# Stick-breaking attention by sigmoids and a scan of products, with the weights' products shared between GpSimd and VectorE

## The reference

```python
for i in range(seq // Q_BLOCK):                       # Q_BLOCK = 128, seq = 512
    z = jnp.einsum('bqhd,bkhd->bhqk', q[:, q0:kv_len], k[:, :kv_len]).astype(jnp.float32) * scale
    causal = k_pos < q_pos
    log_beta = jax.nn.log_sigmoid(z)
    log_1m = jnp.where(causal, log_beta - z, 0.0)
    later = lax.cumsum(log_1m, axis=3, reverse=True) - log_1m
    w = jnp.where(causal, jnp.exp(log_beta + later), 0.0)
    outs.append(jnp.einsum('bhqk,bkhd->bqhd', w.astype(v.dtype), v[:, :kv_len]))
```

## Time and profile before

| | |
|---|---|
| median of 3 runs (lowest, highest) | 1973.13 us (1972.97, 1973.66) |
| the profiled execution, its own time | 1974.07 us |
| its span, from first to last instruction | 1972.3 us |
| TensorE busy | 1940.5 us, 98% |
| VectorE busy | 1470.6 us, 75% |
| ScalarE busy | 953.6 us, 48% |
| GpSimd busy | 454.8 us, 23% |
| mean granted clock of TensorE | 0.997 |

### The profile page before, as it was taken

One profiled execution on the slowest core, in us unless ns is written; L12 is line 12 of the kernel. 1 busy time (PEld: TensorE's weight loads), 2 busy tenths in 40 slices (PEclk: granted clock), 3 DMA queues, 4 the chain that ended last, 5 costly groups with the idle time before them and its releaser, 6 DMA issues.

```text
span 1972.3 us, 27125 instructions
## 1 busy us (share of the span) xinstructions
PE 1940.5 (98%) x10176; PEld 1582.1 (80%) x10176; DVE 1470.6 (75%) x2123; ACT 953.6 (48%) x1541; POOL 454.8 (23%) x471
## 2 busy tenths in 40 slices
PE   9999999999999999999999999999999999999997
PEld 6777878898897776787889889788888888886666
DVE  8995477877785449757786778778778778437985
ACT  5574343333344348733333335565555555236774
POOL 4131100570171000010066036124333331000002
PEclk9999999999999999999999999999999999999998
DMA  8465322243233220022324224322222223322112
GB/s 291 112 140 161 106 77 97 64 145 92 75 108 117 87 95 11 1 88 86 99 75 145 86 70 115 91 71 59 86 85 77 81 65 107 98 79 72 36 38 75
DMA packets 84546, 180.57 MB, mean 92 GB/s; under 512 B 18240, under 2 KB 33984, under 8 KB 84416
## 3 DMA queue, kind: packets, MB, share of 16 engines
q1 hardware_dynamic: 80848, 172.08, 29.1%
q0 software_dynamic: 3424, 6.23, 1.2%
q10 hardware_dynamic: 144, 0.52, 0.1%
HBM read 171.53 MB, written 7.27 MB: 91 GB/s over the span
## 4 chain that ended last, share of the span: by engine, by line
PE 68%; DVE 18%; ACT 6%; issue 6%; DMA 1%; SPq 0%; DVEq 0%; ACTq 0%
PE psum L522 12%; PE psum L525 12%; PE psum L523 12%; DVE wl L418 3%; ACT wh L406 3%; PE psum L462 3%; PE psum L459 3%; PE psum L460 3%; PE psum L563 2%; PE psum L566 2%; PE psum L564 2%; PE psum L544 2%; PE psum L1090 1%; PE psum L1092 1%; PE psum L1091 1%
## 5 line engine op out<-in xcount | busy, mean ns | idle before, releaser
L418 DVE TENSOR_TENSOR wl<-raw,wh 128x1024 fp32r<-128x1024 f32 (+3 forms) x359 | 430.8, 1203 | 255.1 <-ACT wh L406 254.2
L522 PE MATMUL psum<-xh,wh 128*128 128x512 f32 x1376 | 543.2, 395 | 1.8 <-DVE xl L641 1.8
L525 PE MATMUL psum<-xh,wl 128*128 128x512 f32 x1376 | 537.0, 390 | 2.5 <-DVE wl L418 2.5
L523 PE MATMUL psum<-xl,wh 128*128 128x512 f32 x1376 | 535.7, 389 | 0.0
L406 ACT ACTIVATE wh<-raw 128x1024 fp32r<-128x1024 f32 (+3 forms) x359 | 345.0, 964 | 291.1 <-PE psum L525 98.9
L522 PEld LDWEIGHTS psum<-xh,wh 128*128 128x128 f32 x1376 | 258.4, 188 | 61.2 <-ACT wh L406 2.6
L525 PEld LDWEIGHTS psum<-xh,wl 128*128 128x128 f32 x1376 | 258.3, 188 | 60.2 <-DVE wl L418 6.3
L523 PEld LDWEIGHTS psum<-xl,wh 128*128 128x128 f32 x1376 | 258.4, 188 | 55.2 <-issue 2.4
L431 POOL TENSOR_TENSOR raw<-raw 128x256 f32<-128x256 f32 x78 | 74.0, 949 | 441.1 <-DMA raw<-d_w 441.1
L462 PE MATMUL psum<-fh,wl 128*128 128x256 f32 x546 | 154.9, 284 | 1.8 <-DVE wl L418 1.6
L459 PE MATMUL psum<-fh,wh 128*128 128x256 f32 x546 | 154.7, 283 | 1.2 <-DVE fl L965 1.0
(11 more groups left out here) (548 smaller groups left out, 3710.3 us busy)
## 6 DMA issues: line engine op xcount, KB each, us to landing
raw<-d_w SPq DMA_DIRECT2D x224, 512.0 KB, 3.6
raw<-d_w SPq DMA_DIRECT2D x126, 256.0 KB, 2.7
Mt<-d_kd SPq DMA_DIRECT2D x64, 64.0 KB, 2.5
raw<-d_w SPq DMA_DIRECT2D x8, 320.0 KB, 2.9
bc<-d_bc SPq DMA_DIRECT2D x8, 256.0 KB, 4.5
d_ud<-ust SPq DMA_DIRECT2D x8, 256.0 KB, 2.6
U<-d_ud POOLq DMA_DIRECT2D x64, 32.0 KB, 2.4
d_yd<-HY SPq DMA_DIRECT2D x64, 32.0 KB, 2.1
```

Source lines behind the costliest of these rows:

```text
L418: dve.e.tensor_tensor(K.wl[n % NH][:, 0:w], K.raw[n % RAW][:, o:o + w], K.wh[n % NH][:, 0:w].bitcast(F32), ALU.subtract).then_inc(K.S["lo" ...
L522: pe.e.matmul(b[:, :], WH[:, o:o + P], XH, start=(k == k0), stop=False)
L523: pe.e.matmul(b[:, :], WH[:, o:o + P], XL, start=False, stop=False)
L525: mm = pe.e.matmul(b[:, :], WL[:, o:o + P], XH, start=False, stop=(k == k1 - 1))
```

## The change

The attention now has 32 steps n = 4 p + i, one for a pair of heads p and a block of 128 queries i, with queries in the partitions and 128 (i + 1) keys along the row, for both heads. Per step:

- TensorE, `scores_pe(n)`: two products and two masks into banks 0, 1 or 2, 3 in turn, which it may take when the scans of step n - 2 are done ("rem").
- ScalarE, `sigmoid_act(n)`: beta = sigmoid(z) into one of three buffers (the third is `xs`), which it may write when the turn of step n - 3 is done ("trn"); then sigmoid(-z) in place in PSUM.
- VectorE, `remain_dve(n)`: a reversed scan of products over each head's row gives the share left (`left`, two buffers), first head 1, then head 0; then it multiplies beta of head 1 by the share left.
- GpSimd, `weigh_pool(n)`: multiplies beta of head 0 by the share left.
- TensorE, `turn1_pe(n)`: 2 (i + 1) transposes into banks 4 and 5, which it may take when the copy of step n - 1 is done ("wg"). ScalarE, `turned_act(n)`: copies them into `ww` (two buffers). After each fourth turn, `mix_pe(p)` as before.

Sums, splits, absolute values, Exp and Ln are gone. ScalarE loads the table of the sigmoid before step 0, and at t = 4 the table of Ln and Exp for `head_rsqrt_act(3)` and the sigmoid's again; the second FFN starts with the table of Ln and Exp, which before was still loaded from the attention. The queues run through t = 2 to 31 with scores t, turn t - 3 and, where t is divisible by 4, a mix. The last mix stands after five of eight steps of b_w_o.

```diff
-def sums_pe(K, pe, p, part):
...
-def softplus_act(K, act, i):
...
-def weigh_act(K, act, i):
...
-def softplus_abs_dve(K, dve, p):
...
-def softplus_dve(K, dve, i):
...
+TURN_BANK, SPREAD_BANK = 4, 6
+def score_bank(n):
+    return 2 - n % 2 * 2
+def keys(n):
+    return P * (n % 4 + 1)
+def scores(K, n):
+    b = score_bank(n)
+    return K.psum[:, b:b + 2, 0:keys(n)]
+def beta(K, n):
+    return K.beta[n % 3].rearrange("p (e c) -> p e c", e=2)[:, :, 0:keys(n)]
...
+def scores_pe(K, pe, n):
+    p, i = n // 4, n % 4
     pe.wait_ge("kq", 8 + p + 1)
+    pe.wait_ge("mk", 4)
     for e in range(2):
+        take(pe, score_bank(n) + e, ("rem", 2 * n + 1))
+    for e in range(2):
+        r = slice(64 * e, 64 * e + 64)
+        pe.e.matmul(scores(K, n)[:, e, :], K.qT[r, p, i * P:(i + 1) * P], K.kT[r, p, 0:keys(n)], start=True, stop=False,
+                    skip_group_check=True)
+    for e in range(2):
+        mm = pe.e.matmul(scores(K, n)[:, e, i * P:(i + 1) * P], K.mkb[:, :], K.idb[:, :], start=False, stop=True,
                          skip_group_check=True)
     mm.then_inc(K.S["sc"], 1)
+def sigmoid_act(K, act, n):
+    z = scores(K, n)
+    act.wait_ge("sc", n + 1)
+    act.wait_ge("trn", n - 2)
+    act.other("sigmoid")
+    act.e.activation(beta(K, n), z, ACT.Sigmoid).then_inc(K.S["act"], act.up())
+    act.e.activation(z, z, ACT.Sigmoid, scale=-1.0).then_inc(K.S["sgm"], 1)
+def remain_dve(K, dve, n):
+    z, out = scores(K, n), K.left[n % 2]
+    dve.wait_ge("sgm", n + 1)
+    dve.wait_ge("wgt", n - 1)
+    dve.wait_ge("mk", 4)
+    k = keys(n)
+    none = K.zero[:, 0:1].broadcast_to([P, k])
+    dve.e.tensor_tensor_scan(out[:, 1, 0:k][:, ::-1], z[:, 1, :][:, ::-1], none, 1.0, ALU.mult, ALU.add).then_inc(
+        K.S["dve"], dve.up())
+    scanned = dve.n
+    dve.e.tensor_tensor_scan(out[:, 0, 0:k][:, ::-1], z[:, 0, :][:, ::-1], none, 1.0, ALU.mult, ALU.add).then_inc(
+        K.S["rem"], 1)
+    dve.wait_ge("dve", scanned)
+    w = beta(K, n)[:, 1, 0:k - 1]
+    dve.e.tensor_tensor(w, w, out[:, 1, 1:k], ALU.mult).then_inc(K.S["rem"], 1)
+def weigh_pool(K, pool, n):
+    k = keys(n)
+    w = beta(K, n)[:, 0, 0:k - 1]
+    pool.wait_ge("rem", 2 * n + 1)
+    pool.e.tensor_tensor(w, w, K.left[n % 2][:, 0, 1:k], ALU.mult).then_inc(K.S["wgt"], 1)
+def turn1_pe(K, pe, n):
     for e in range(2):
+        take(pe, TURN_BANK + e, ("wg", n + 1))
+    pe.wait_ge("wgt", n + 1)
+    pe.wait_ge("rem", 2 * n + 2)
     for e in range(2):
+        for j in range(n % 4 + 1):
+            c = slice(j * P, (j + 1) * P)
+            mm = pe.e.transpose(K.bank[TURN_BANK + e][:, c], beta(K, n)[:, e, c], K.con("ident"))
+    mm.then_inc(K.S["trn"], 1)
+def turned_act(K, act, n):
+    p, i = n // 4, n % 4
+    act.wait_ge("trn", n + 1)
+    act.wait_ge("mix", p - 1)
+    act.wait_ge("hbc", 16)
+    act.e.activation(K.ww[:, p % 2, :, i:4 * i + 1:3, :],
+                     K.psum[:, TURN_BANK:TURN_BANK + 2, 0:keys(n)].rearrange("p e (j c) -> p e j c", c=P),
+                     ACT.Copy).then_inc(K.S["wg"], 1)
...
 def att1_pe(K, pe):
...
+    for t in range(2, 32):
+        scores_pe(K, pe, t)
+        if t == 2:
             head_sums_pe(K, pe, 3, 7)
+        if t in LATE_HEADS:
+            head_spread_pe(K, pe, 3, LATE_HEADS[t], SPREAD_BANK)
+        if t >= 3:
+            turn1_pe(K, pe, t - 3)
+        if t % 4 == 0 and t >= 8:
+            mix_pe(K, pe, t // 4 - 2)
+    turn1_pe(K, pe, 29)
     x = x_of(K, pe, 5)
     last = product_steps(K, pe, "b_w_o", (0, 1), (2, 3), x, (("h", 17), ("h", 18)))
+    next(last)
+    turn1_pe(K, pe, 30)
+    mix_pe(K, pe, 6)
+    next(last)
+    next(last)
+    turn1_pe(K, pe, 31)
+    next(last)
+    next(last)
     mix_pe(K, pe, 7)
...
 def att1_act(K, act):
...
+    for t in range(2, 35):
+        if t < 32:
+            sigmoid_act(K, act, t)
+        if t == 4:
             head_rsqrt_act(K, act, 3)
+        if t >= 3:
+            turned_act(K, act, t - 3)
+        if t % 4 == 1 and t >= 9:
+            mixed_act(K, act, t // 4 - 2)
     mixed_act(K, act, 7)
```

More of the change, by code:

```diff
@@ L345 @@
     + ["gcp", "conv", "fa", "gv", "fh", "fl"]
-    + ["hcp", "hsq", "hn", "hny", "hbc", "kq", "mk", "sc", "sp2", "spa", "spl", "sums", "wg", "mix", "vt"]
+    + ["hcp", "hsq", "hn", "hny", "hbc", "kq", "mk", "sc", "sgm", "rem", "wgt", "trn", "wg", "mix", "vt"]
     + ["mraw", "dtk", "mxs", "mset", "mseta", "msetp", "mci", "mcv", "mth", "mfin", "mz", "mzt", "mcbp", "mcb", "mtp", "mxt"]
@@ L1271, in sums_pe @@
     for e in range(2):
-        pe.e.matmul(z[:, e, :], own, A[0][:, e, :], start=False, stop=False, skip_group_check=True)
-    pe.wait_ge("spl", i + 3)
-    for e in range(2):
-        mm = pe.e.matmul(z[:, e, :], own, A[1][:, e, :], start=False, stop=True, skip_group_check=True)
-    mm.then_inc(K.S["sums"], 1)
+        for j in range(n % 4 + 1):
+            c = slice(j * P, (j + 1) * P)
+            mm = pe.e.transpose(K.bank[TURN_BANK + e][:, c], beta(K, n)[:, e, c], K.con("ident"))
+    mm.then_inc(K.S["trn"], 1)
@@ L1309, in weigh_act @@
-def weigh_act(K, act, i):
-    act.wait_ge("sums", i + 1)
-    act.wait_ge("mix", i // 3)
-    act.wait_ge("hbc", 16)
-    act.e.activation(part_of(K.ww, i), part_psum(K, i), ACT.Exp).then_inc(K.S["wg"], 1)
 def mixed_act(K, act, p):
@@ L1375, in att1_pe @@
         product(K, pe, "b_w_q", n - 8, 4 + n % 4, x, ("hcp", n + 1),
[L1376 removed]
+                between=(2, lambda K, pe: scores_pe(K, pe, 0)) if n == 14 else None)
         if n == 12:
@@ L1512, in att1_pool @@
 def att1_pool(K, pool):
+    for n in range(32):
+        weigh_pool(K, pool, n)
     add_squares(K, pool, 3)
@@ L3418, in att1_tensors @@
     K.Vt["w_kv"] = sb("Vt", [P, 4, D])
-    K.tri = sb("tri", [P, 2, P], R32)
-    K.ww = sb("ww", [P, 2560])
     K.idb = sb("idb", [P, P], BF16)
     K.mkb = sb("mkb", [P, P], BF16)
-    K.t0 = sb("t0", [P, 1024])
-    K.t1 = sb("t1", [P, 1024])
-    K.hsq = [t[:, o:o + T] for t in (K.t0, K.t1) for o in (0, T)]
-    K.hsq += [K.ww[:, o:o + T] for o in range(0, 4 * T, T)]
-    spare = (UNIT[("b_w_o", "T", 0, 0)] + 2) % NH
-    K.sp = [[(sb("sph0", [P, 1024], R32), sb("spl0", [P, 1024], R32)), (K.wh[spare], K.wl[spare])],
-            [(sb(f"sph1{i}", [P, T], R32), sb(f"spl1{i}", [P, T], R32)) for i in range(2)],
-            (sb("sph2", [P, 1024], R32), sb("spl2", [P, 1024], R32))]
+    K.zero = sb("zero", [P, 1])
+    K.left = [sb(f"left{i}", [P, 2, T]) for i in range(2)]
+    K.beta = [sb(f"beta{i}", [P, 2 * T])[:, :] for i in range(2)] + [K.T]
+    ww = sb("ww", [P, 2, 2, 13, P])
+    K.ww = ww[:, :, :, :, :]
+    whole = K.ww.rearrange("p r e b c -> p (r e b c)")
+    K.hsq = [whole[:, o:o + T] for o in range(0, 8 * T, T)]
 def mamba_tensors(K, sb):
```

200 lines of the change are left out of this document (23 added, 177 removed).

## The result

The changed kernel takes 2012.82 us (median of 4 runs, 2011.78 to 2013.86) beside 1973.24 for the kernel before: a ratio of 1.0200, 95% interval 1.0183 to 1.0218, so **39.6 us slower**. The forecast was 1993.4 in a range of 1985 to 2005: the right side, and half of the size.

A forecast was written before the change was run, and what follows sets the result against it. The prediction took a ring of waits between TensorE's turns and ScalarE's sigmoids and copies to bound the loop, 13.4 us per pair against 10.92. Its terms gave +20.3 us on the median 1973.13: 1993.4 us, range 1986 to 2003 (1985 to 2005 with rival 2).

The forecast's parts named there:

- The ring: Attention loop: turn, two sigmoids, copy, next turn wait on each other without overlap; period 13.4 us per pair against 10.92.
- the term for T: Turn transposes on TensorE in one round of four steps: 3.9 us plus releases by the copy, 4.1; lower end 3.3.
- the mix with scores in the ring: Once a pair, mix and next scores stand on TensorE between two turns; adds 1.7 us to the period.
- T(0): First turn by transposes on TensorE, forecast to start at 748.1 us, after scores, head sums and scores of 3.5.
- one round: Four steps of the loop, turns 4.1, sigmoids 5.2 and copies 2.4: 11.7 us, without the mix.
- rival 3: TensorE's clock falls to half in the loop and tail; about 2045 us, chance 9%.
- once PEclk is under 1.0 for more than a few us: Sign in the loop that would decide for TensorE's clock falling, about 2045 us.
- the prediction's step 5: Sum's fifth term: at loop step 4 ScalarE's last rsqrt, table loads and wait for VectorE's mean cost 5.5 us.
- cost at nothing: Scores' wait for the scans of two steps before, taken as 0 unless scans end over 1 us later.
- Rival 1: Turns run while ScalarE does sigmoids, busy time decides, period under 10.9 us; 1965 us, chance 6%.
- Rival 2: GpSimd takes the shared ports first, its 3.5 us adding to VectorE's 9.2; 1993 to 1999 us, chance 12%.
- TensorE near 65% busy: Sign that the forecast is right: TensorE's busy share in the attention loop.

The follow-up runs named there:

- e12: Changed kernel plus unused TensorE products in most steps, six of 512 columns in steps 4 to 6, none in steps 7, 10, 11, 14; 1997.78 us.
- e6: Changed kernel without the second head's scan; that head is multiplied by the first one's share; 2010.31 us.
- e3: Changed kernel plus unused TensorE products ahead of the turns of steps 4 to 6 and from 15 on; 2001.19 us.
- e2: Changed kernel with a fourth beta buffer, so sigmoids of step t wait for the turn of t - 4; 1981.09 us.
- e13: Changed kernel with four beta buffers, 1 - beta in SBUF by GpSimd (ScalarE in steps 6 to 13), scan zeros mostly in PSUM, last norm's mean earlier; 1967.44 us.
- e5: Changed kernel with both heads' products on VectorE, GpSimd doing nothing in the loop; 2012.36 us.
- e9: Changed kernel plus unused TensorE products spread over all steps, ten of 512 columns in steps 4 to 6; 2005.87 us.
- e11: Changed kernel with four beta buffers, GpSimd making 1 - beta in SBUF, scan zeros mostly in PSUM, seven unused TensorE products around steps 5 and 6; 1980.97 us.

## Why the prediction was half right

**The ring** was read rightly from the order, and its price holds. One period of e12, from the mix at 824.37 to the next, TensorE and ScalarE:

```profile
824.37 2.37 PE L1276 MATMUL psum<-ww,Vt 128*64 128x512 f32 x16
824.54 0.38 ACT L1202 ACTIVATE beta<-psum 128x256 f32<-128x256 f32 x1 [0.81 <-PE psum L1253]
824.82 0.38 ACT L1203 ACTIVATE psum<-psum 128x256 f32<-128x256 f32 x1
825.12 0.59 ACT L1263 ACTIVATE ww<-psum 128x512 f32<-128x512 f32 x1
826.67 0.70 PE L1188 MATMUL psum<-kT,qT 64*128 64x256 f32 x4
...
827.43 0.82 PE L1253 MATMUL psum<-con,beta 128*128 128x128 f32 x6
...
828.35 0.60 ACT L1202 ACTIVATE beta<-psum 128x512 f32<-128x512 f32 x1 [2.65 <-PE psum L1253]
...
829.36 0.80 ACT L1263 ACTIVATE ww<-psum 128x768 f32<-128x768 f32 x1
...
830.22 0.86 PEld L1253 LDWEIGHTS psum<-con,xs 128*128 128x128 f32 x8 [0.81 <-ACT ww L1263]
830.22 1.09 PE L1253 MATMUL psum<-con,xs 128*128 128x128 f32 x8 [0.41 <-ACT ww L1263]
...
831.41 0.81 ACT L1202 ACTIVATE xs<-psum 128x768 f32<-128x768 f32 x1 [0.76 <-PE psum L1253]
...
832.84 1.02 ACT L1263 ACTIVATE ww<-psum 128x1024 f32<-128x1024 f32 x1
...
833.91 0.44 PE L1253 MATMUL psum<-con,beta 128*128 128x128 f32 x2 [0.41 <-ACT ww L1263]
834.45 1.02 ACT L1202 ACTIVATE beta<-psum 128x1024 f32<-128x1024 f32 x1 [0.59 <-PE psum L1253]
...
836.31 0.38 ACT L1263 ACTIVATE ww<-psum 128x256 f32<-128x256 f32 x1
...
836.74 0.66 PE L1253 MATMUL psum<-con,beta 128*128 128x128 f32 x4 [0.31 <-ACT ww L1263]
837.33 1.08 PE L1276 MATMUL psum<-ww,Vt 128*64 128x512 f32 x4
```

Read from start to start: turn to sigmoid 0.92 + 1.19 + 0.54 and, from the start of the turn at 836.74 to a sigmoid at 837.50, 0.76, together 3.4 (forecast 4.1, its low end 3.3; but the reason given for the low end isn't what happens: the first weight load starts with the first transpose, both at 830.22, and not behind the scores ahead of the wait); sigmoids to copy 0.58 + 1.01 + 1.43 + 1.86 = 4.9 (5.2); copy to turn 0.86 + 1.07 + 0.43 and, of the 2.31 from the copy at 825.12 to the turn at 827.43, an estimated 0.64 for the copy, 3.0 (2.4, releases in the term for T); and the other 1.67 for the mix with scores in the ring (1.7). Sum 12.96 (13.4).

**By stages**, in us, the clock's part, after less e12, being taken from two kernels of which one has fillers:

| | forecast | e12 | after | clock |
|---|---|---|---|---|
| start of the first mix | 768.9 | 768.99 | 772.44 | 3.5 |
| first to sixth mix | 67.0 | 68.3 | 78.8 | 10.4 |
| sixth to eighth mix | 24.2 | 25.5 | 27.7 | 2.2 |
| end of the last mix | 862.4 | 865.1 | 881.2 | 16.1 |

(The forecast's first mix: T(0) at 748.1, one round 11.7, the next step 2.9, step 4's 5.5 and four transposes 0.7.) Of the 19.4 us by which the forecast was too low (1993.4 for 2012.8), 15.0 (at least) are the clock's and 4.4 are left at e12. Against e12's trace the sum is short by 2.7 us; the rest is between profiled executions and medians. Two pieces can be named. The spreads of the last heads' norm (L1138, 1.1 us each, four of them between scores and turns of steps 7 to 13) are in no term: the first two periods of e12 are 14.6 and 14.8 where the later ones are 12.96. The period's own excess of 0.4 paid part of that back. And in the tail the b_w_o step behind T(29) took 2.7 us at the low clock instead of 1.4.

**The failed step is the clock**: the sum priced every stretch of TensorE at the high clock, with no term for a part of the loop at the low one, and left the clock to rival 3, put at 9%. That rival had it fall for the whole loop or not at all, 2045 or nothing, and its price was too high by its own terms (2.4 + 3.2 + 0.5 are 6.1 us per pair, not 7.5). The prediction said what decides ("once PEclk is under 1.0 for more than a few us"), but didn't ask which waits of the loop's first steps would bring that about. There it fell: TensorE works for 1.21 us in 752 to 757, PEclk is 0.64 in them and 0.50 behind. The fall itself came at 753.4, ahead of TensorE's wait of 3.07 us for step 4 (the prediction's step 5) and behind three shorter ones, two of which are the scores' waits for scans that the prediction "cost at nothing". It doesn't need those: in e6, with one scan less, it falls at 751.8, before the scores of step 5 begin, behind a wait of 1.75 us for a copy. Nor is the wait of step 4 without a part: in e3, with fillers ahead of it, the clock fell within that wait. What exactly in what TensorE does makes it fall stays open. Once low, it makes the turns, scores and mixes in the ring longer, so the periods grow to 17.0, and it comes and goes for the rest of the loop. That the falls are a cause and no mere companion is shown by e3 and e12, where TensorE does more and the kernel is 11.6 and 15.0 us faster. By how much fillers delay turns themselves isn't known, so 15 us is a lower bound of the clock's part. The Trainium skill, "TensorE: Matmul & The Clock Gate" (PE-mode transpose), holds that a transpose does not count as busy as a product does. Whether the falls came from the transposes or from the idle time no run here tells; the fillers were ordinary products and filled idle time at once.

**Rival 1** (the ring cut, 1965) fell, as both waits held. As a kernel it exists: e2 cuts the ring and has a period of 10.7, under the 10.9 that the rival names, and e13, with 9.1 where its 9.2 us of VectorE work promised 9.2, takes 1967.4. **Rival 2** fell with e5. GpSimd's products took 1.45 us for 511 columns beside VectorE's, where 1.28 stood in the earlier trace rows, and VectorE's own weren't longer than forecast but in the narrowest (127 columns 0.27 to 0.53 for 0.29). **The other prices held**: scan from PSUM 1.224 for 1.224, sigmoid to PSUM 1.018 for 1.02, copy 1.019, GpSimd 0.44 and 1.09 for 127 and 383 columns. The wait of scores for scans, put at nothing, came to 4.4 us of TensorE's time in all (5.3 of its weight loads). e6, with one scan less, returns 2.5 us in all, so little of it lay outside the ring's shadow. "TensorE near 65% busy" came out at 107.07 of 139, 77%, at least in part because half-clock instructions count as busy for twice as long: a busy share doesn't show work where the clock moves.

## What to carry to other kernels

Where queues are in order and buffers single, write the loop of waits down and add it up beside the busy sums: here four engines under 11 us per pair made a ring of 13, and one more buffer was worth 31.7 us, with what it gave back of the clock. Where a change leaves TensorE idle, even in a few short waits at one place, price the clock as a term with a part of the loop, not as a rival of all or nothing: here the low clock made the ring longer, and the ring's idle time went with further falls. And before filling idle time, look at what the filler waits for and what is queued behind it (e9, e11).
